# A fused two-block transformer kernel: the first map of each differential head left unscaled, its squared sum in the norm, and the tile norm's pieces moved

## What is computed

```python
sc = jnp.where(mask, sc, NEG_INF)                      # two score maps per head
p = jax.nn.softmax(sc, axis=-1)
a = (p[:, :, 0] - lam * p[:, :, 1]).astype(v.dtype)
o = jnp.einsum('bhqk,bkhd->bqhd', a, v)
...
o = rms_norm(o, subln_g) * (1.0 - lam_init)            # over a head's 64 columns, RMS_EPS = 1e-6
```

## Time and profile before

| what | us |
| --- | --- |
| median of 3 runs | 1066.6 |
| lowest and highest of them | 1064.37, 1069.93 |
| the profiled execution's own time | 1064.1 |
| its span, first instruction to last | 1062.3 |
| engine busy: PE, DVE, ACT, POOL | 1014.8, 599.7, 531.8, 413.6 |
| mean granted clock of TensorE, share of full | 0.987 |

### The profile page before, as it was taken

The page is one execution under the profiler, slowest core; times in us unless marked ns, Lnnn a source line. Parts: engine busy times, 40 slices in busy tenths (PEclk is TensorE's granted clock), DMA queues, the critical chain, the costliest instruction groups (busy, mean ns, idle before and its releaser), DMA issues.

```text
span 1062.3 us, 14972 instructions
## 1 busy us (share of the span) xinstructions
PE 1014.8 (96%) x5118; PEld 826.4 (78%) x5118; DVE 599.7 (56%) x1305; ACT 531.8 (50%) x1090; POOL 413.6 (39%) x235
## 2 busy tenths in 40 slices
PE   6999999999999999999999999999999989977898
PEld 4779888888778788888888888778888768844667
DVE  4547367988455566454454545432224989776632
ACT  5443656877434344444444444543334465777721
POOL 2456412000144444444444444414443334455432
PEclk9999999999999999999999999999999999998899
DMA  7564222111134322222222224342353214343123
GB/s 252 200 167 151 96 81 75 51 41 40 41 99 139 119 99 82 97 99 99 99 99 98 96 84 146 103 137 101 106 179 110 69 70 139 93 113 93 55 75 118
DMA packets 38810, 111.86 MB, mean 105 GB/s; under 512 B 5235, under 2 KB 8563, under 8 KB 38067
## 3 DMA queue, kind: packets, MB, share of 16 engines
q1 hardware_dynamic: 28572, 87.60, 25.3%
q10 hardware_dynamic: 8584, 18.89, 5.5%
q0 software_dynamic: 1600, 4.66, 1.2%
HBM read 100.25 MB, written 7.96 MB: 102 GB/s over the span
## 4 chain that ended last, share of the span: by engine, by line
issue 49%; PE 23%; POOL 14%; DVE 7%; ACT 3%; DMA 3%; POOLq 0%; ACTq 0%; DVEq 0%
POOL WLO L674 13%; PE PS L1902 6%; PE PS L1904 6%; PE PS L1903 6%; DMA RAW<-wstream 2%; PE PS L2093 1%; PE PS L2074 1%; PE PS L2269 1%; DMA X<-xT 1%; POOL PB L742 1%; ACT WHI L768 1%; DVE FX L1706 1%; ACT PB L937 0%; DVE FX L1702 0%; DVE X L1401 0%
## 5 line engine op out<-in xcount | busy, mean ns | idle before, releaser
L674 POOL TENSOR_TENSOR WLO<-RAW,WHI 128x1024 fp32r<-128x1024 f32 x147 | 355.5, 2419 | 571.2 <-ACT WHI L768 571.1
L768 ACT ACTIVATE WHI<-RAW 128x1024 fp32r<-128x1024 f32 x154 | 162.8, 1058 | 271.7 <-PE PS L1904 250.9
L1902 PE MATMUL PS<-HHI,WHI 128*128 128x512 f32 x648 | 256.2, 395 | 10.2 <-DVE HLO L1297 9.2
L1903 PE MATMUL PS<-HLO,WHI 128*128 128x512 f32 x648 | 253.5, 391 | 0.0
L1904 PE MATMUL PS<-HHI,WLO 128*128 128x512 f32 x648 | 253.5, 391 | 0.0
L1902 PEld LDWEIGHTS PS<-HHI,WHI 128*128 128x128 f32 x648 | 122.5, 189 | 39.7 <-issue 12.3
L1902 PE MATMUL PS<-BHI,WHI 128*128 128x512 f32 x368 | 145.8, 396 | 4.8 <-DVE BLO L1319 2.8
L1904 PE MATMUL PS<-BHI,WLO 128*128 128x512 f32 x368 | 143.5, 390 | 0.0
L1903 PE MATMUL PS<-BLO,WHI 128*128 128x512 f32 x368 | 143.3, 389 | 0.0
L1904 PEld LDWEIGHTS PS<-HHI,WLO 128*128 128x128 f32 x648 | 122.3, 189 | 25.8
L1903 PEld LDWEIGHTS PS<-HLO,WHI 128*128 128x128 f32 x648 | 122.5, 189 | 25.2 <-issue 0.5
(11 more groups left out here) (333 smaller groups left out, 1474.3 us busy)
## 6 DMA issues: line engine op xcount, KB each, us to landing
RAW<-wstream SPq DMA_DIRECT2D x154, 512.0 KB, 3.2
X<-xT ACTq DMA_DIRECT2D x4, 512.0 KB, 9.7
BF<-wstream POOLq DMA_DIRECT2D x2, 1024.0 KB, 6.8
BG<-wstream POOLq DMA_DIRECT2D x2, 1024.0 KB, 7.5
bias_b<-bias_rows ACTq DMA_DIRECT2D x2, 1024.0 KB
FX<-bias_b ACTq DMA_DIRECT2D x8, 256.0 KB, 2.5
X<-xT ACTq DMA_DIRECT2D x8, 256.0 KB, 3.6
x_keep<-X ACTq DMA_DIRECT2D x2, 1024.0 KB, 6.4
```

The costliest lines, as they stand in the source:

```text
L674: pool.tensor_tensor(WLO[:, s, :], RAW[:, s, :], WHI[:, s, :].bitcast(F), ALU.subtract).then_inc(split_lo, 1)
L768: act.activation(WHI[:, c % 2, :], RAW[:, c % 2, :], ACT.Copy).then_inc(split_hi, 1)
L1902: pe.matmul(dst, a[0], b[0], start=first, stop=False, **kw)
L1903: pe.matmul(dst, a[0], b[1], start=False, stop=False, **kw)
```

## The change

1. A hold map is no longer multiplied. `normed` returns at once for it, and POOL's four multiplications, the hold's reciprocal and the semaphores `first_sums` and `first_held` are gone. The sub map's weight is instead minus lambda times the first map's row sum S over the second's, so that the sum is S times what it was. The norm removes the factor S if EPS is multiplied by S squared; one added instruction per sub map writes that (`eps_of`), and the mean square takes it as its second input.
2. POOL's low half of unit wout2 + 1 comes after map 4 and no longer after map 5.
3. The two scalings of tile 0 on DVE and its high half on ACT move from step 12 to step 13, its low half on DVE to the end of step 14's maps part. Tile 1 stays at step 18. (The spread on PE and the copy of the roots on ACT stay at steps 12 and 18.)
4. On PE the column sums come ahead of the transposes of the step. In steps 4 and 10 (`AHEAD`) the scores of map i + 3 are also issued, behind the column sums where there are any, and so ahead of the product; in steps 5 and 11 no scores remain to be issued.

```diff
+        DIFF_OUT = [m + 6 - t_ for t_, m in enumerate(DIFF_AT)]
+        def out_tile(i):
+            return DIFF_OUT.index(i) if i in DIFF_OUT else None
+        def eps_of(tile):
+            return SS[:, 32 + 8 * tile:40 + 8 * tile]
...
# POOL
-                elif m.get("mode") == "hold":
-                    pool.wait_ge(first_sums, m["h"] + 1)
-                    for q in range(NT):
-                        ap = prob_of(m, q)
-                        ins = pool.tensor_scalar(ap, ap, stat(m, WT)[:, q:q + 1], None, ALU.mult)
-                    ins.then_inc(first_held, 1)
...
-                if m["i"] == 5:
+                if m["i"] == 4:
                     low_halves(UNIT["wout2"] + 1, UNIT["wout2"] + 2)
# ACT, ahead of the tile's high half
+                    tile = out_tile(i) if name == "late" else None
# DVE, normed
+                if m.get("mode") == "hold":
+                    return
                 dve.wait_ge(A["exped"], m["i"] + 1)
...
-                if m.get("mode") == "hold":
-                    dve.reciprocal(stat(m, WT), stat(m, SUM)).then_inc(first_sums, 1)
-                    return
...
                 if m.get("mode") == "sub":
-                    link(dve.tensor_tensor(stat(m, WT), stat(m, WT), LAM[:, 0:1].broadcast_to([P, NT]), ALU.mult))
-                if m.get("mode") == "sub":
-                    dve.wait_ge(first_held, m["h"] + 1)
+                    first = stat(m["prev"], SUM)
+                    dve.scalar_tensor_tensor(out=eps_of(m["h"] // 2)[:, m["h"] % 2::2], in0=first, scalar=EPS, in1=first,
+                                             op0=ALU.mult, op1=ALU.mult)
+                    link(dve.scalar_tensor_tensor(out=stat(m, WT), in0=stat(m, WT), scalar=LAM[:, 0:1], in1=first,
+                                                  op0=ALU.mult, op1=ALU.mult))
# DVE, attention
-                    tile = diff_tile(maps, i - 5)
+                    if name == "late" and i == DIFF_OUT[0] + 1:
+                        dve.wait_ge(dm_hi, 1)
+                        low_from_psum(lo(Y_DM), hi(Y_DM), YT).then_inc(dm_lo, 1)
+                    tile = out_tile(i) if name == "late" else None
...
-                    if tile is not None:
-                        dve.wait_ge(dm_hi, tile + 1)
-                        low_from_psum(lo(Y_DM + tile), hi(Y_DM + tile), YT).then_inc(dm_lo, 1)
+                    if tile == 1:
+                        dve.wait_ge(dm_hi, 2)
+                        low_from_psum(lo(Y_DM + 1), hi(Y_DM + 1), YT).then_inc(dm_lo, 1)
...
-                        link(dve.tensor_scalar(SS[:, 0:8], PS[:, SUM_BANK[tile], 0:8], 1.0 / 64, EPS, ALU.mult, ALU.add))
+                        link(dve.scalar_tensor_tensor(out=SS[:, 0:8], in0=PS[:, SUM_BANK[tile], 0:8], scalar=1.0 / 64,
+                                                      in1=eps_of(tile), op0=ALU.mult, op1=ALU.add))
# PE, attention
-                    if 0 <= i + 2 < len(maps) and (name, i) != ("late", 0):
+                    if name == "late" and i and i + 2 < len(maps) and i - 1 not in AHEAD:
+                        scores(A, maps[i + 2])
+                    if diff_tile(maps, i - 3) is not None:
+                        tile = diff_tile(maps, i - 3)
+                        pe.wait_ge(dm_sq, tile + 1)
+                        for tk in range(NT):
+                            ins = pe.matmul(PS[:, SUM_BANK[tile], 2 * tk:2 * tk + 2], YSQ[:, tk * P:(tk + 1) * P], BONE[:, 0:P:64],
+                                            start=True, stop=True, skip_group_check=True)
+                        ins.then_inc(dm_tot, 1)
+                    if name == "late" and i in AHEAD:
+                        scores(A, maps[i + 3])
+                    if name == "ab" and i + 2 < len(maps):
                         scores(A, maps[i + 2])
...
-                    if diff_tile(maps, i - 3) is not None:
-                        tile = diff_tile(maps, i - 3)
-                        pe.wait_ge(dm_sq, tile + 1)
...
+            AHEAD = [m["i"] for m in LATE if m.get("mode") == "hold" and m["prev"].get("end") and "latent" in m["prev"]]
```

6 lines of the change are left out of this document (1 added, 5 removed).

## The result

| what | before | after |
| --- | --- | --- |
| median of the runs taken side by side, us | 1068.26 (4 runs) | 1057.32 (4 runs) |
| lowest and highest | 1064.37, 1070.18 | 1052.88, 1058.3 |
| the profiled execution's own time | 1064.1 | 1052.88 |
| its span | 1062.3 | 1050.9 |
| mean granted clock in it | 0.987 | 0.994 |

The ratio is 0.9895, with a 95% interval of 0.986 to 0.9929: faster, by 10.9 us. The forecast was 1057.7 us. In a second series the ratio was 0.990 [0.9871, 0.993]. All ten runs of the changed kernel have a median of 1056.1, all runs of the kernel before in this study one of 1066.0, so the gain is best taken as 9.9 us.

A forecast was written before the change was run, and what follows sets the result against it. It held that the late attention's end counts, ahead of a fixed projection tail, with no engine full and three handing maps around. Terms 2.7 + 1.9 + 0 + 3.4 + 0.9 = 8.9 us off 1066.6 gave 1057.7 us, range 1052.5 to 1062.5.

The forecast's parts named there:

- faster: Whole kernel: a measurement tells it faster than before, beyond about 0.5% or 5.3 us; chance 0.82.
- first and second head pair, hold unscaled: Sub maps 5 and 7: subtractions no longer wait for POOL, the first not doubled; 2.7 and 1.9 us gained.
- sub map 11: Its wait for POOL is 0.36 us, but the path there runs over ACT: counted 0.
- tile 0 a step later: From product 9's end to `biased` of 15: 8.5 us where it took 11.8; 3.4 us gained at product 13.
- column sums ahead: Step 16: tile 1's sums run in PE's 2.15 us hole, product 15 starts 0.9 us sooner.
- scores ahead, as schedule: Scores of maps 7 and 13 ahead of products 3 and 9: 0; for 13, bounds -0.6 and +0.4 us.
- the low half's move to step 4: POOL's low half runs earlier, keeping its 2.36 us off map 5's subtraction, which then takes 1.94 us, not 3.96.
- The clock, a rival: Products 7, 9 and 15 all run at 2.4 GHz: 4.3 us more, 13.2 in all, 1053.4 us; chance 0.17.
- a sign of being wrong: Half clock under products 3 or 13 would show the prediction wrong.
- Part of it is given back: Clock drops fall on product 13 and two latent maps' scores: 5.1 us gained, 1061.5 us; chance 0.18.
- Hides anyway: Steps 5 and 7 didn't wait for the hold's scaling; only tile and sums count, some 3 us; chance 0.06.
- Slower: PE's waits for `biased` keep 1.2 GHz from product 3 to the projection: some 16 us cost, 1073.7; chance 0.04.

The follow-up runs named there:

- second series: The changed kernel run again, unaltered, on the chip of the three kernels with one part each: 1055.42 us (6 runs), ratio 0.990.
- filled kernels: Unused matmuls put into TensorE's idle times: kernel before (76) 1062.46 us, changed kernel (30) 1050.31, changed kernel with TensorE's old order (62) 1056.00.
- order back: Changed kernel with part 4 undone, column sums behind the transposes and scores in steps 5 and 11: 1063.17 us; with 62 unused matmuls 1056.00.
- filled kernel after: Changed kernel plus 30 unused matmuls in TensorE's idle times in steps 8, 10, 14 and 16: 1050.31 us (4 runs), ratio 0.9855.
- tile taken back: Changed kernel with part 3 undone, tile 0's scalings, high and low half in step 12 again: 1056.53 us (6 runs), ratio 0.9905.

## Why the prediction was right, and where it was not

**The number.** 1057.7 forecast, 1057.3 and 1055.4 measured in the two series; 8.9 us forecast, 9.9 over all runs. For the profiled execution 1055.2 was forecast and 1052.9 measured. The case "faster" came in, the range held.

**The terms**, against the schedule at full clock (the filled kernels, and the same with the added matmuls' delays taken off):

| term | forecast | filled kernels | delays off |
| --- | --- | --- | --- |
| first and second head pair, hold unscaled | 2.7 + 1.9 | 4.25 | 4.7 |
| sub map 11 | 0 | 0.46 | 0.0 |
| tile 0 a step later | 3.4 | 3.53 | 3.5 |
| column sums ahead | 0.9 | 1.22 + 1.11 | 0.8 + 1.1 |
| scores ahead, as schedule | 0 | 0.15 | -0.2 |
| sum | 8.9 | 10.7 | 9.9 |

- **Hold.** Right in size and in its reasoning: line 1523 of map 3 (now L1532) comes at 7.97 us from the gate product of map 1, which is 942.7 in the time of the profile before, against 942.75 forecast. The 2.7 of 3.8 that arrive are so because the product of map 3 sets the rest. Wrong was one reason: the low half's move to step 4 was credited with clearing the subtraction, and the run without the move shows the same 1.94. Product 7 ended at 22.36 us, 957.1 in the time of the profile before, where 959.1 was forecast: the forecast carried the half clock of the kernel before along (product 7 at 28.96 there, at 27.02 filled).
- **Tile.** Right as a schedule: `biased` of 15 starts at 976.21, 8.3 us behind product 9's end at 967.89, against 8.5 forecast. What the working didn't say is that most of this term exists only with the hold's part in (alone 1.4 in the medians and 0.5 in the profile, with a wait of 2.33 in its place).
- **Column sums.** The mis-sized term. "What follows product 15 depends on it, not on them" was read from a trace in which product 15 was slow. At full clock POOL's chain behind the sums comes last, and the term is 1.9: the 0.9 that was counted, measured as 0.8, and 1.1 that was put at nothing.
- **Scores ahead.** "They run in PE's 2.65 us hole and cost nothing" is right for the schedule: nothing at product 3 and 0.2 us at product 9, within the stated bounds. As an account of what this part is worth it failed: without it the kernel is 5.2 us slower. Since the schedule shows no such gain and the clock in the attention falls from 0.95 and 0.98 to 0.85, this is put down to the clock; the kernel without scores ahead was not itself filled, but the one with the whole order back was, and got its 7.2 us back.

**The clock, a rival priced at 13.2 us in all with a chance of 0.17.** In the profiled execution it is what happened: 13.5 us, no product slow. In the second profile of the same kernel two products were slow, the first of them map 3's, which the prediction had named as a sign of being wrong, and the attention was 10.6 us shorter. What was set against it ("the place of a drop can't be read off the hole before it", the first drop not agreeing) was not strong enough. The slow product of map 7 in the profile before came well behind a hole, but with the hold unscaled, the mean clock follows the holes: 0.985 with the scores behind, 0.991 ahead (0.990 and 0.992 in the two series), 0.996 with fillers. With nothing but TensorE's order changed, the scores ahead didn't move it. By the Trainium skill, TensorE: Matmul & The Clock Gate, "What's actually happening", throttled is the default and activity releases it; the filled kernels agree, since extra matmuls are all that was added to them.

**Why the number came out.** The schedule at full clock is worth 9.9 us by its terms, 1.0 more than the sum, and this is POOL's chain. What the change gains or loses by the clock beside that is small in the net. The kernel before loses 5.0 us to half clock (1066.0 less the 1062.5 of the filled one, and the 1.4 that the added matmuls cost this one), since other waits covered part of its slow work. The kernel after loses 6.0 (1056.1 less 1050.3, and 0.2), although it has less half clock. The filled medians, 12.15 us apart, are 10.9 apart with the delays off, and 10.9 less 1.0 is the 9.9 measured. These last terms are differences of medians and hold chance in the stretch ahead of the attention, so that no more can be said than that the net is near nothing. The prediction had left the clock out of its sum, and that the losses before and after nearly cancel is luck: without the scores ahead the same kernel is at 1061.3, 4.7 us faster than before and not 9.9.

**The other rivals.** "Part of it is given back" (5.1) is what the change gives with the scores not ahead: 1061.3. "Hides anyway" fell with the filled kernels, where the hold is worth 4.7 us (alone, 4.6 in the medians and 2.2 at like clock). "Slower" didn't come near; its mechanism exists, but in the opposite direction, since the waits of TensorE for `biased` (0.43, 0.31, 0.84) are shorter than the idle times that they break up.

**Open.** The start of the late attention varies from execution to execution by up to 8 us among all the profiles (932.5 to 940.5), in a part of the program that all of them share; what moves it was not looked for. It is of the size of most differences between the medians here, so a median of 4 or 6 runs can be off by some of it: the tile taken back shows 3 us and more in a profile and 0.4 in the medians, and of the filled kernel after's 5.8 us its profiles show 0.1 to 3.0 in the attention. Nor was it tried which of TensorE's idle times decides a drop of the clock: one at a time was not filled.

## What to carry to other kernels

Where TensorE waits two or three microseconds for another engine ahead of a large product, put independent matmuls there, later work first and idle matmuls if there is none, and read the granted clock of the stretch behind it: here the scores of two maps, moved ahead of a product, were worth 5 us, and 30 matmuls without use up to 6 more, of which part lies in a stretch that they don't touch. Keep such a group shorter than the wait, or its own delay has to be taken off before terms are compared. Read the waits behind a slow instruction with care: what it hides is a term of its own once it runs at full speed. And price parts of a change together where one part's wait is the other's cover: alone these gave 6.4 us, together 10.4. Where a stretch ahead of the change varies by as much as the change is worth, compare the changed stretch in several profiles, counted from one instruction, and not only the medians.

## What the runs showed of the hardware that was not expected

- More work made each of three kernels faster in the medians: 76 unused matmuls 3.6 us, 30 unused matmuls 5.8 us, 62 unused matmuls 7.2 us. In the attention alone the profiles show 2.3, 0.1 to 3.0, and 9.0.
- Half clock has no fixed price. It follows from what else sets the path. Against the same schedule at full clock, with the added matmuls' delays off, the attention lost 3.7 us at a clock of 0.88 (before: 83.1, estimated 79.4), 3.2 at 0.95 (after, second series: 72.5, estimated 69.3) and 10.4 at 0.83 (order back: 81.4, estimated 71.0).
- One kernel's executions differ in where half clock falls: the two profiles of the kernel after have 0.98 and 0.95 in the attention, and products 3 and 9 at full speed in one and slow in the other.
- A DVE instruction on 4 columns was blocked for 2.34 us by POOL, as long as POOL's 1024-column one ran, while the one ahead of it, started 0.02 us before POOL, took its normal 0.17.
